# Attention layer of a fused two-block kernel: the query and key norms take their roots in batches of four tiles, from raw tiles copied out of PSUM, and the steps of an attention unit stand further apart

## The chip, the cores and the metric

One Trainium2 chip, one of its cores. The metric is the device time of one execution of the whole program in microseconds (us), measured from the outside; the kernel before was run three times. The profile and the trace come from a fourth, profiled execution. The program is one instruction stream for each engine: TensorE (PE in the rows, its weight loads PEld), VectorE (DVE), ScalarE (ACT), GpSimd (POOL) and SyncE (SP). They run side by side and meet at semaphores only; each takes its own instructions strictly in order.

## What is computed

The reference runs two transformer blocks after each other on 256 tokens of 1024 numbers, in float32. The first has a recurrent mixer, sliding-window attention and a mixture of experts. The second has two layers: feed-forward, mixer, feed-forward, each with a residual. The mixer of its second layer is the dilated attention that the change touches. What matters of it, in short form:

```
qkv = rmsnorm(h) @ w_qkv            # 256 x 1024 times 1024 x 9216: 3 groups of q, k, v with 16 heads of 64
for g, dilation in enumerate((1, 4, 16)):
    q = q_g * rsqrt(mean(q_g ** 2, over the 64 of a head) + eps) * q_gain[g]
    k = k_g * rsqrt(mean(k_g ** 2, over the 64 of a head) + eps) * k_gain[g]
    scores = q k^T * 64 ** -0.5 + bias        # the banded keys that the group's dilation reaches
    o_g, lse_g = softmax(scores) @ v_g, logsumexp(scores)
o = sum over g of softmax_g(lse_g) * o_g
mix = o @ w_out
```

## The kernel before, in words

**The work as a whole.** Every dense layer is cut into tiles of 128 or 256 output columns. Weights come from HBM in float32, one megabyte a transfer, on SyncE's queue. ScalarE rounds each tile of weights to its high part (`hi_tile`, L324), VectorE subtracts that from the tile for the low part (`lo_tile`, L328), and TensorE multiplies high and low parts in separate passes. There are four slots of split weights (`SLOTS_W`).

**The attention layer** (`attention_mixer`, L1891) has the layer `qkv` of 72 tiles. One tile is 128 tokens by 256 output columns, that is four heads; tiles 2i and 2i + 1 share their weights and are the two halves of the tokens. A tile takes 8 chunks of three matmuls (L387, L388, L389) and stays in one of three PSUM banks. The 16 heads are worked off in four turns of four heads. A turn is 18 tiles: 12 query and key tiles (three groups, query and key, two halves of the tokens) and 6 value tiles. `query(t)` numbers the 48 query and key tiles n = 0 to 47.

**A query or key tile**, before: ScalarE squares it out of PSUM (`square`, L2007, scaled by the token's root), VectorE sums the squares of each head (`sum_squares`, L2202), ScalarE takes the root (`root`, L2011), VectorE the reciprocal (`invert_root`, L2207) and then multiplies the tile in PSUM by the token's and the head's factors (`normalise`, L2196) into one of four SBUF buffers QNR. That frees the PSUM bank: `bank_free` lets TensorE begin tile t + 3 when tile t is normalised. TensorE turns the normalised tile (`transposes`, L2096, two instructions) three tiles later, and ScalarE takes the turned tile into QK (`take`, L2001). Value tiles are copied out of PSUM by ScalarE (`take_values`, L2017, L2021).

**An attention unit** is two heads and one half of the queries; there are four in a turn. Its steps are scores (TensorE, L2106 and L2114), bias and maximum (VectorE, L2219), exp (ScalarE, L2030), scaling of the even and the odd head's weights (VectorE, L2229 and L2230), turning each (TensorE, L2125), taking each (ScalarE, L2038), weighing the values (TensorE, L2138), and for every second unit the high and low parts of the output (`out_high` on ScalarE, L2050, `out_low` on VectorE, L2242).

**What sets the order.** Nothing is scheduled by a planner: each engine's order comes out of `run_layer` (ScalarE and VectorE) and `products` (TensorE), and the steps of the attention units are put in by tables. A step's place is counted in chunks of TensorE from the start of its turn, `BEGIN + APART * q + offset`: the scores of unit 0 stand at chunk 124 (tile 15 of the turn, chunk 4), the next units 12 chunks further each. `PE_STEPS`, `DVE_STEPS` and `ACT_STEPS` (L1914 to L1916) give the offsets. The units reach over the end of their turn into tiles 0 to 4 of the next one; those of the last turn reach into the output layer `attn_out`, whose chunks come from `LAST_BEFORE`.

In `run_layer`, for each tile of this layer:

```
work(t)                       # evacuation; the steps at place 0 of VectorE follow
if t is odd: make(n + 3)      # a high split on ScalarE, a low split on VectorE
between(t)                    # steps at the middle place
if t is odd: make(n + 4)
behind(t)                     # steps at the last place
```

Both high splits of an odd tile wait for the matmuls of that tile, since these read the slots that are written.

## Time and profile before

| | us |
|---|---|
| three runs, median (lowest, highest) | 2464.3 (2457.86, 2464.69) |
| the profiled execution, its own time | 2468.32 |
| span of the profiled execution, first to last instruction | 2466.4 |
| busy in the span: TensorE | 2351.7 |
| VectorE | 1340.3 |
| ScalarE | 1010.1 |
| GpSimd | 94.8 |
| the attention layer's matmuls, first to last start | 1946.7 to 2232.2 |

The trace has a row for each instruction: its start, how long it took, the engine, the line of the program, the operation, what it writes and reads, and in brackets how long the engine had been idle and what ended that. Times of the trace count from the span's start. Table loads of ScalarE (ACT_TABLE_LOAD) have rows of their own. A row with x2 or more is a run of equal instructions. TensorE's instructions overlap: a matmul begins before the one before it ends, so the cost of many is read from their starts.

### The profile page before, as it was taken

How to read it: one execution, taken by the hardware profiler on the slowest of the kernel's cores; microseconds unless marked ns; L12 is line 12 of the kernel's file. 1: busy time of each engine (PE TensorE's matmuls, PEld its weight loads, DVE VectorE, ACT ScalarE, POOL GpSimd, SP SyncE). 2: the span in 40 equal slices, each digit the busy share in tenths (PEclk: the TensorE clock that was granted, in tenths of full speed). 3: DMA queues.
4: the chain of work that ended last, by engine and by line, in shares of the span. 5: the costliest groups of instructions: out<-in, count | busy, mean ns of one | idle time of the engine just before them, and what ended most of it. 6: DMA issues, size and time to landing. Idle time of an engine off the chain costs nothing.

```text
span 2466.4 us, 36862 instructions
## 1 busy us (share of the span) xinstructions
PE 2351.7 (95%) x13979; PEld 1647.8 (67%) x13980; DVE 1340.3 (54%) x2641; ACT 1010.1 (41%) x1832; POOL 94.8 (4%) x150
## 2 busy tenths in 40 slices
PE   6999999999999999999989999999999899999999
PEld 3777854444444444444448888888888788887888
DVE  5688752222232222223247869877777555665784
ACT  3645541111111111111136546655555576775653
POOL 1000000000000000000000000000000210011000
PEclk8999999999999999999999999999999999999999
DMA  8754679999999999999975556555555655453553
GB/s 318 250 208 151 235 287 424 426 426 425 425 425 425 425 425 425 425 425 426 426 291 188 181 179 200 175 188 175 183 188 176 188 151 157 143 162 120 176 181 121
DMA packets 279032, 673.89 MB, mean 273 GB/s; under 512 B 8884, under 2 KB 236607, under 8 KB 246016
## 3 DMA queue, kind: packets, MB, share of 16 engines
q1 hardware_dynamic: 274656, 663.60, 71.1%
q0 software_dynamic: 4256, 8.65, 1.6%
q8 instruction: 80, 1.31, 0.2%
q14 instruction: 40, 0.33, 0.0%
HBM read 670.45 MB, written 1.25 MB: 272 GB/s over the span
## 4 chain that ended last, share of the span: by engine, by line
PE 83%; DVE 6%; ACT 5%; DMA 4%; issue 3%; DVEq 0%; ACTq 0%; SPq 0%
PE PS L380 26%; PE PS L1493 17%; PE PS L381 13%; PE PS L1515 9%; PE PS L1480 5%; DMA RING<-in_moe_w 3%; PE PS L1467 2%; PE PS L387 2%; PE PS L389 2%; PE PS L388 2%; DVE WS L328 1%; ACT WS L324 1%; DVE XG L1610 1%; PE PS L798 1%; DMA RAW<-in_w_ada 1%
## 5 line engine op out<-in xcount | busy, mean ns | idle before, releaser
L380 PE MATMUL PS<-HN,WS 128*128 128x512 f32 x1952 | 707.0, 405 | 15.4 <-DVE WS L328 9.4
L328 DVE TENSOR_TENSOR WS<-RAW,WS 128x1024 fp32r<-128x1024 f32 (+1 forms) x452 | 540.9, 1205 | 172.6 <-ACT WS L324 168.9
L381 PE MATMUL PS<-HN,WS 128*128 128x256 f32 x1952 | 551.7, 283 | 0.0
L324 ACT ACTIVATE WS<-RAW 128x1024 fp32r<-128x1024 f32 (+1 forms) x452 | 465.0, 1035 | 83.2 <-PE PS L381 69.5
L1493 PE MATMUL PS<-RING,XG 128*64 128x512 f32 x2048 | 447.2, 594 | 12.3 <-DVE XG L1610 11.0
L380 PEld LDWEIGHTS PS<-HN,WS 128*128 128x128 f32 x1952 | 371.1, 190 | 111.3 <-DVE WS L328 11.6
L381 PEld LDWEIGHTS PS<-HN,WS 128*128 128x128 f32 x1952 | 373.5, 191 | 0.3
L1493 PEld LDWEIGHTS PS<-RING,XG 128*64 128x64 f32 x2048 | 148.8, 137 | 296.2 <-issue 292.1
L1616 DVE TENSOR_SCALAR GLU<-PS 128x256 f32<-128x256 f32 x64 | 27.2, 425 | 415.2 <-PE PS L1493 415.2
L380 PE MATMUL PS<-MI,WS 128*128 128x512 f32 x704 | 248.9, 399 | 0.0
L1515 PE MATMUL PS<-RING,AT 128*64 128x512 f32 x1024 | 226.8, 594 | 14.8 <-ACT AT L1389 14.8
L1382 ACT ACTIVATE SIG<-GLU 128x256 f32<-128x256 f32 x64 | 26.7, 417 | 520.9 <-DVE GLU L1616 520.9
L381 PE MATMUL PS<-MI,WS 128*128 128x256 f32 x704 | 197.7, 281 | 0.0
L387 PE MATMUL PS<-WS,HN 128*128 128x256 f32 x576 | 172.0, 299 | 7.8 <-DVE QNR L2196 4.1
L1515 PEld LDWEIGHTS PS<-RING,AT 128*64 128x64 f32 x1024 | 84.6, 137 | 136.4 <-issue 135.4
L388 PE MATMUL PS<-WS,HN 128*128 128x256 f32 x576 | 163.9, 285 | 0.0
L389 PE MATMUL PS<-WS,HN 128*128 128x256 f32 x576 | 163.7, 284 | 0.0
L380 PEld LDWEIGHTS PS<-MI,WS 128*128 128x128 f32 x704 | 132.3, 188 | 33.0
L1480 PEld LDWEIGHTS PS<-PSEL,H2K 128*128 128x128 f32 x1024 | 116.7, 192 | 25.9 <-issue 25.2
L381 PEld LDWEIGHTS PS<-MI,WS 128*128 128x128 f32 x704 | 133.0, 189 | 0.0
L1610 DVE TENSOR_TENSOR XG<-PS,SH 128x512 f32<-128x512 f32 x32 | 22.1, 692 | 200.9 <-PE PS L1480 200.9
L1480 PE MATMUL PS<-PSEL,H2K 128*128 128x64 f32 x1024 | 121.1, 276 | 0.3 <-DVE PGAT L1605 0.3
(361 smaller groups left out, 2705.2 us busy)
## 6 DMA issues: line engine op xcount, KB each, us to landing
RING<-in_moe_w SPq DMA_DIRECT2D x192, 2048.0 KB, 22.7
RAW<-in_ffn_w_in SPq DMA_DIRECT2D x88, 1024.0 KB, 5.2
RAW<-in_attn_w_qkv SPq DMA_DIRECT2D x36, 1024.0 KB, 5.2
RAW<-in_ffn_w_out SPq DMA_DIRECT2D x32, 1024.0 KB, 5.0
RAW<-in_w_ada SPq DMA_DIRECT2D x24, 1024.0 KB, 8.1
RAW<-in_w_in SPq DMA_DIRECT2D x22, 1024.0 KB, 5.3
RAW<-in_ffn_w_out SPq DMA_DIRECT2D x16, 768.0 KB, 4.3
RAW<-in_conv_w_in SPq DMA_DIRECT2D x12, 1024.0 KB, 5.2
```

The costliest lines, as they stand in the source:

```text
L324: act_f(split_tile(0, n), raw_tile(n), ACT.Copy).then_inc(hi_done, 1)
L328: vec.tensor_tensor(split_tile(1, n), raw_tile(n), split_tile(0, n).bitcast(f32), ALU.subtract).then_inc(lo_done, 1)
L380: nc.tensor.matmul(both, hi[:, k, :], x2[:, :, kx, :], start=start, stop=False)
L381: ins = nc.tensor.matmul(half, lo[:, k, :], x2[:, 0, kx, :], start=False, stop=stop)
L387: nc.tensor.matmul(half, xh, w2[:, 0], start=start, stop=False)
L388: nc.tensor.matmul(half, xh, w2[:, 1], start=False, stop=False)
L389: ins = nc.tensor.matmul(half, xl, w2[:, 0], start=False, stop=stop)
L1467: nc.tensor.matmul(bank[COMB[m]][:, :], PGT[64 * g:64 * g + 64, tt * P:(tt + 1) * P], YE[64 * g:64 * g + 64, :], start=True, stop=True).th ...
L1480: last = nc.tensor.matmul(bank[4][:, k * SLOTS:(k + 1) * SLOTS], H2K[:, tt, k * P:(k + 1) * P], PSEL[:, tt, :], start=tt == 0, stop=tt == ...
L1493: last = nc.tensor.matmul(bank[j][64 * side:64 * side + 64, :], XG[:, 2 * q + k, :], w[:, k, 1024 * side + 512 * j:1024 * side + 512 * (j ...
L1515: last = nc.tensor.matmul(bank[6][64 * side:64 * side + 64, :], AT[:, b, 64 * q:64 * q + 64], w[:, b, 512 * side:512 * (side + 1)], start= ...
L1610: TTN(XG[:, :, :], bank[4][:, :].rearrange("p (k s) -> p k s", k=DC), SH2[:, :].rearrange("p (k a) -> p k a", a=1).to_broadcast([P, DC, SL ...
```

## The change

- Before, each query or key tile had its own root and its own reciprocal, of 4 columns each. Now four tiles make a batch (`BATCH = 4`), with one root and one reciprocal of 16 columns (`roots`, `invert_roots`).
- VectorE copies a tile out of PSUM as soon as its matmuls are done (`take_raw`), scaled by the token's root; that frees the bank. ScalarE squares the copy, in SBUF, in `between`, and VectorE sums in `behind`. `normalise` multiplies the copy in place in SBUF by the heads' factors. There are eight QNR buffers in place of four.
- The turning of a batch that ends with tile t comes behind tile t + 1 (first half) and tile t + 2 (second half); before, each tile was turned three tiles later.
- ScalarE runs an exp of one column behind tile 12 of each turn.
- The offsets of a unit's steps grow: the key turns by 2 chunks, the weighing by 3, the scalings by 1, the copies by 2, the output parts by 3. The scores, bias and exp stay.

```diff
-        QNR = [rg(f"QNR{i}", [S]) for i in range(4)]
-        QST = rg("QST", [4, 4])
-        QSI = rg("QSI", [2, 4])
-        RSE = rg("RSE", [TT])
+        QNR = [rg(f"QNR{i}", [S]) for i in range(2 * BATCH)]
+        QST = rg("QST", [2, BATCH, 4])
...
-        PE_STEPS = {"scores": 0, "turn_even": 12, "turn_odd": 15, "weigh": 20}
-        DVE_STEPS = {"bias": 0, "scale_even": 8, "scale_odd": 10, "out_low": 23}
-        ACT_STEPS = {"exp": 5, "take_even": 13, "take_odd": 16, "out_high": 22}
+        PE_STEPS = {"scores": 0, "turn_even": 14, "turn_odd": 17, "weigh": 23}
+        DVE_STEPS = {"bias": 0, "scale_even": 9, "scale_odd": 11, "out_low": 26}
+        ACT_STEPS = {"exp": 5, "take_even": 15, "take_odd": 18, "out_high": 25}
...
+        def batch_end(t):
+            n = query(t)
+            return n // BATCH if n is not None and n % BATCH == BATCH - 1 else None
+
+        def turned_at(s):
+            j, first = batch_end(s - 1), 0
+            if j is None:
+                j, first = batch_end(s - 2), BATCH // 2
+            return [] if j is None else [BATCH * j + first + i for i in range(BATCH // 2)]
...
-                pe.wait_ge(sem("q_normed"), n + 1)
+                pe.wait_ge(sem("q_raw"), n + 1)
...
-            def square(n, t):
+            def square(n):
                 if n >= 2:
                     act.wait_ge(sem("q_summed"), n - 1)
-                act.wait_ge(mm_done, qkv.end[t])
-                act_f(QSQ[n % 2][:, :], tile_bank(qkv, t), ACT.Square, scale=RSE[:, t % 2:t % 2 + 1]).then_inc(sem("q_sq"), 1)
-
-            def root(n):
-                act.wait_ge(sem("q_summed"), n + 1)
-                act_f(QST[:, n % 4, :], QST[:, n % 4, :], ACT.Sqrt, bias=EPSC[:, 0:1]).then_inc(sem("q_root"), 1)
+                act.wait_ge(sem("q_raw"), n + 1)
+                act_f(QSQ[n % 2][:, :], QNR[n % (2 * BATCH)][:, :], ACT.Square, scale=HD ** -0.5).then_inc(sem("q_sq"), 1)
+
+            def roots(j):
+                act.wait_ge(sem("q_summed"), BATCH * (j + 1))
+                st = QST[:, j % 2, :, :]
+                act_f(st, st, ACT.Sqrt, bias=EPSC[:, 0:1]).then_inc(sem("q_root"), 1)
...
             def behind(s):
-                n = query(s - 3)
-                if n is not None:
+                for n in turned_at(s):
                     take(n)
                 c, w = turn_and_tile(s)
                 if c >= 0:
                     for kind, q in ACT_AT.get((w, 1), ()):
                         step(c, kind, q)
+                j = batch_end(s)
+                if j is not None:
+                    roots(j)
 
             def between(s):
                 n = query(s)
                 if n is not None:
-                    root(n)
+                    square(n)
+                if s % TURN_TILES == TURN_Q:
+                    act_f(STAT[:, 6, 0:1], EPSC[:, 0:1], ACT.Exp)
...
-                n = query(s - 3)
-                if n is not None:
+                for n in turned_at(s):
                     transposes(n)
...
-            def normalise(n, t):
-                dve.wait_ge(sem("q_inverse"), n + 1)
-                if n >= 4:
-                    dve.wait_ge(sem("q_T"), n - 3)
-                heads = "p (h d) -> p h d"
-                STT(QNR[n % 4][:, :].rearrange(heads, h=4), tile_bank(qkv, t).rearrange(heads, h=4), token_root(t),
-                    QSI[:, n % 2, :].rearrange("p (h a) -> p h a", a=1).to_broadcast([P, 4, HD]),
-                    ALU.mult, ALU.mult).then_inc(sem("q_normed"), 1)
+            def normalise(n):
+                raw = QNR[n % (2 * BATCH)][:, :].rearrange("p (h d) -> p h d", h=4)
+                dve.wait_ge(sem("q_inverse"), n // BATCH + 1)
+                dve.wait_ge(sem("q_raw"), n + 1)
+                TTN(raw, raw, QST[:, n // BATCH % 2, n % BATCH, :].rearrange("p (h a) -> p h a", a=1).to_broadcast([P, 4, HD]),
+                    ALU.mult).then_inc(sem("q_normed"), 1)
+
+            def take_raw(n, t):
+                if n >= 2 * BATCH:
+                    dve.wait_ge(sem("q_T"), n - 2 * BATCH + 1)
+                dve.wait_ge(mm_done, qkv.end[t])
+                TS(QNR[n % (2 * BATCH)][:, :], tile_bank(qkv, t), token_root(t), None, ALU.mult).then_inc(sem("q_raw"), 1)
...
             def behind(s):
-                steps_at(s, 2)
                 n = query(s)
                 if n is not None:
-                    invert_root(n)
+                    sum_squares(n)
+                steps_at(s, 2)
+                j = batch_end(s - 1)
+                if j is not None:
+                    for n in range(BATCH * j + BATCH // 2, BATCH * (j + 1)):
+                        normalise(n)
 
             def work(t):
...
-                n = query(t - 1)
-                if n is not None:
-                    normalise(n, t - 1)
+                j = batch_end(t - 1)
+                if j is not None:
+                    invert_roots(j)
+                    for n in range(BATCH * j, BATCH * j + BATCH // 2):
+                        normalise(n)
                 n = query(t)
                 if n is not None:
-                    sum_squares(n)
+                    take_raw(n, t)
```

How the engines' orders move at the places of which the prediction speaks (no times in them; L numbers are the lines of the version shown, those of the new one differ by up to 24):

**VectorE, quiet tiles, before**: query tiles 6 and 7 of turn 0 (`L2202` the sum, `L2207` the reciprocal, `L2196` the multiplication out of PSUM, `L328` the two low splits behind the odd tile).

```order
L2202 TENSOR_REDUCE QST<-QSQ_168 128x4 [waits q_sq]
L2207 RECIPROCAL QSI<-QST 128x4 [waits q_root]
L2196 SCALAR_TENSOR_TENSOR QNR_172<-PS,RSC,QSI 128x256 [waits q_T,q_inverse]
L2202 TENSOR_REDUCE QST<-QSQ_169 128x4 [waits q_sq]
L328 TENSOR_TENSOR WS<-RAW_66,WS 128x1024 [waits hi_done] x2
L2207 RECIPROCAL QSI<-QST 128x4 [waits q_root]
L2196 SCALAR_TENSOR_TENSOR QNR_173<-PS,RSC,QSI 128x256 [waits q_T,q_inverse]
```

**VectorE, the same place, now**: `L2214` is the raw copy, `L2220` the sum, `L2226` the batch's reciprocal, `L2207` the multiplication in SBUF. QNR_177 holds tile 7, the last of its batch.

```order
L2214 TENSOR_SCALAR QNR_177<-PS,RSC 128x256 [waits mm_done]
L328 TENSOR_TENSOR WS<-RAW_66,WS 128x1024 [waits hi_done] x2
L2220 TENSOR_REDUCE QST<-QSQ_169 128x4 [waits q_sq]
L2226 RECIPROCAL QST<-QST 128x16 [waits q_root]
L2207 TENSOR_TENSOR QNR_174<-QNR_174,QST 128x256 [waits q_raw,q_inverse]
L2207 TENSOR_TENSOR QNR_175<-QNR_175,QST 128x256 [waits q_raw,q_inverse]
L2214 TENSOR_SCALAR QNR_170<-PS,RSC 128x256 [waits mm_done,q_T]
L2220 TENSOR_REDUCE QST<-QSQ_168 128x4 [waits q_normed,q_sq]
L2207 TENSOR_TENSOR QNR_176<-QNR_176,QST 128x256 [waits q_raw,q_inverse]
```

The sum of tile 7 has moved from ahead of the two low splits to behind them; the batch's reciprocal and multiplications come after it.

**TensorE behind tile 8 of turn 0, before**: the turning of tile 5 (QNR_171), between the last matmuls of tile 8 and the first of tile 9.

```order
L388 MATMUL PS<-WS,HN 128x256
L389 MATMUL PS<-WS,HN 128x256
L2096 MATMUL PS<-SM,QNR_171 128x128 [waits q_taken,q_normed]
L2096 MATMUL PS<-SM,QNR_171 128x128
L387 MATMUL PS<-WS,HN 128x256 [waits q_normed]
```

**TensorE behind tile 8, now**: the turning of tiles 4 and 5 (QNR_174, QNR_175), the first half of the batch that ends with tile 7.

```order
L389 MATMUL PS<-WS,HN 128x256
L2109 MATMUL PS<-SM,QNR_174 128x128 [waits q_taken,q_normed]
L2109 MATMUL PS<-SM,QNR_174 128x128
L2109 MATMUL PS<-SM,QNR_175 128x128 [waits q_taken,q_normed]
L2109 MATMUL PS<-SM,QNR_175 128x128
L387 MATMUL PS<-WS,HN 128x256 [waits q_raw]
```

Two tiles are turned there in place of one, and both wait for multiplications that need the sum of tile 7, which is one tile back.

**ScalarE where turn 0 runs into turn 1 (tiles 18 to 21), before**: `L2038` takes turned weights, `L2007` squares, `L2030` is the exp, `L2011` the root.

```order
L2038 ACTIVATE ETX_179<-PS 128x384 [waits b_pv,b_T]
L2007 ACTIVATE QSQ_168<-PS,RSE 128x256 [waits mm_done,q_summed]
L2011 ACT_TABLE_LOAD
L2011 ACTIVATE QST<-QST,EPSC 128x4 [waits q_summed]
L2038 ACTIVATE ETX_180<-PS 128x384 [waits b_pv,b_T]
L2030 ACT_TABLE_LOAD
L2030 ACTIVATE ES_177,STAT<-ES_177,STAT 128x384 [waits b_max] x2
L2050 ACTIVATE OXB<-PS 128x256 [waits b_pv]
L2007 ACTIVATE QSQ_169<-PS,RSE 128x256 [waits mm_done,q_summed]
L324 ACTIVATE WS<-RAW_68 128x1024 [waits mm_done,raw_loaded3]
L2011 ACT_TABLE_LOAD
L2011 ACTIVATE QST<-QST,EPSC 128x4 [waits q_summed]
```

**ScalarE, the same place, now**: `L2050` takes turned weights, `L2018` squares the raw copy, `L2042` is the exp, `L2062` the output's high part, `L2023` the batch's root.

```order
L324 ACTIVATE WS<-RAW_68 128x1024 [waits mm_done,raw_loaded3]
L2042 ACTIVATE ES_180,STAT<-ES_180,STAT 128x384 [waits b_max] x2
L2050 ACTIVATE ETX_182<-PS 128x384 [waits b_pv,b_T]
L2018 ACTIVATE QSQ_168<-QNR_176 128x256 [waits q_raw,q_summed]
L2050 ACTIVATE ETX_181<-PS 128x384 [waits b_pv,b_T]
L324 ACTIVATE WS<-RAW_65 128x1024 [waits mm_done,raw_loaded0]
L2018 ACTIVATE QSQ_169<-QNR_177 128x256 [waits q_raw,q_summed]
L2050 ACTIVATE ETX_182<-PS 128x384 [waits b_pv,b_T]
L324 ACTIVATE WS<-RAW_65 128x1024 [waits mm_done,raw_loaded0]
L2023 ACT_TABLE_LOAD
L2023 ACTIVATE QST<-QST,EPSC 128x16 [waits q_summed]
```

The table loads between the exps are gone; one stands ahead of the batch's root. The copy of the odd head's weights has moved behind the exp of the next unit.

## Rows read from the trace of the kernel before

**Rows 1.** Busy time by stretch: us of it, each engine busy, PEclk, DMA, GB/s.
```profile
1967.00:2001.00 34.00, 34.00 (x288) 34.00 (x287) 22.67 (x38) 22.69 (x45) 0.00 (x0) 1.00 0.51 162
...
2074.00:2115.00 41.00, 34.52 (x358) 30.87 (x357) 22.63 (x54) 30.98 (x57) 10.31 (x16) 1.00 0.56 142
```

**Rows 2.** Timeline, quiet tiles: start us, us, engine, line, operation [idle before].
```profile
1977.78 0.38 PE L2096 MATMUL PS<-SM,QNR 128*128 128x128 f32 x2
...
1978.12 0.28 PE L388 MATMUL PS<-WS,HN 128*128 128x256 f32 x1
...
1980.87 0.38 PE L2096 MATMUL PS<-SM,QNR 128*128 128x128 f32 x2
...
1978.04 0.47 ACT L2007 ACTIVATE QSQ<-PS,RSE 128x256 f32<-128x256 f32 x1 [0.74 <-PE PS L389]
...
1978.41 1.05 ACT L324 ACTIVATE WS<-RAW 128x1024 fp32r<-128x1024 f32 x1
...
1979.36 0.29 ACT L2011 ACTIVATE QST<-QST,EPSC 128x4 f32<-128x4 f32 x1
...
1979.49 2.37 DVE L328 TENSOR_TENSOR WS<-RAW,WS 128x1024 fp32r<-128x1024 f32 x2 [0.53 <-ACT WS L324]
```

**Rows 3.** Timeline, start of the attention layer, the first tile's chain.
```profile
1957.70 0.17 DVE L2265 RECIPROCAL RSC<-RSC 128x2 f32<-128x2 f32 x1 [6.28 <-ACT RSC L2073]
...
1958.61 0.42 DVE L2202 TENSOR_REDUCE QST<-QSQ 128x4 f32<-128x256 f32 x1 [0.54 <-ACT QSQ L2007]
...
1959.06 0.30 ACT L2011 ACTIVATE QST<-QST,EPSC 128x4 f32<-128x4 f32 x1 [0.49 <-DVE QST L2202]
...
1959.39 0.18 DVE L2207 RECIPROCAL QSI<-QST 128x4 f32<-128x4 f32 x1 [0.36 <-ACT QST L2011]
...
1959.60 0.48 DVE L2196 SCALAR_TENSOR_TENSOR QNR<-PS,RSC,QSI 128x256 f32<-128x256 f32 x1
...
1960.14 0.58 PE L387 MATMUL PS<-WS,HN 128*128 128x256 f32 x1 [4.11 <-DVE QNR L2196]
```

**Rows 4.** One line's instructions (L427): ns min/median/max.
```profile
L427 DVE TENSOR_TENSOR DXT<-PS,DXT x8: 414/420/440, 2252.3 to 2270.8; 128x256 f32<-128x256 f32 x8
```

**Rows 5.** Groups by line, 1940 to 2240: busy us, mean ns, idle before.
```profile
L2030 ACT ACT_TABLE_LOAD x10 | 12.8, 1283 | 0.2
```

**Rows 6.** Timeline, TensorE and ScalarE at the end of turn 1.
```profile
2074.19 0.70 PE L2106 MATMUL PS<-QK 64*128 64x256 f32 x4
...
2079.00 1.28 ACT L2030 ACT_TABLE_LOAD   x1
...
2080.30 0.61 ACT L2030 ACTIVATE ES<-ES,STAT 128x384 f32<-128x384 f32 x1
...
2081.72 0.55 PE L2125 MATMUL PS<-SM,EN 128*128 128x128 f32 x3 [0.90 <-DVE EN L2230]
...
2084.39 0.55 PE L2125 MATMUL PS<-SM,EN 128*128 128x128 f32 x3 [1.06 <-DVE EN L2230]
...
2087.82 0.89 PE L2138 MATMUL PS<-ETX,VV 128*64 128x128 f32 x16 [1.09 <-issue]
...
2096.22 0.89 PE L2138 MATMUL PS<-ETX,VV 128*64 128x128 f32 x16 [1.18 <-ACT ETX L2038]
...
2107.69 0.55 PE L2125 MATMUL PS<-SM,EN 128*128 128x128 f32 x3 [1.46 <-DVE EN L2230]
```

**Rows 7.** Gaps of TensorE, and stretches behind gaps with their granted clock.
```profile
1484.73 0.50 PE L380 MATMUL PS<-HN,WS 128*128 128x512 f32 x1 [1.90 <-DVE WS L328]
...
1485.00:1491.00 6.00, 6.00 (x36) 5.25 (x36) 5.83 (x11) 2.79 (x5) 0.00 (x0) 1.00 0.56 175
...
2285.05 0.50 PE L380 MATMUL PS<-HN,WS 128*128 128x512 f32 x1 [1.75 <-DVE WS L328]
...
2285.00:2291.00 6.00, 5.96 (x25) 5.17 (x26) 5.90 (x10) 5.10 (x10) 0.00 (x0) 0.72 0.48 160
...
1960.00:1966.00 6.00, 5.86 (x30) 5.86 (x31) 4.33 (x9) 2.79 (x6) 0.00 (x0) 0.55 0.98 200
```

22 lines of the change are left out of this document (11 added, 11 removed).

## The prediction

> **What bounds the kernel now.** I read the views in this order: busy time by stretch of the attention layer, the timeline of TensorE, ScalarE and VectorE in a quiet stretch of it, then the timeline at the end of a turn, then the granted clock behind long gaps of TensorE.
>
> The layer has 72 tiles, 18 to a turn. In the stretches where only query, key and value tiles run, TensorE has no gap at all; in the 41 us around a turn's end, where the four attention units are threaded in, it is busy 34.52 us and idle 6.48, and ScalarE is busy 30.98 [rows 1]. So a quiet tile costs its matmuls, and any new wait of TensorE there is paid in full; at a turn's end there is something to gain, three times (a fourth end runs into the output layer).
>
> A quiet tile with its two transposes takes 1980.87 - 1977.78 = 3.09 us; the two transposes take 0.21 of it (three matmuls are 0.36 apart, eight times: 2.88) [rows 2]. After an odd tile ScalarE squares it and makes two high splits, 0.95 apart, and VectorE's low splits start 1.08 after the high ones and take 1.18 each in a row [rows 2].
>
> **The new wait, step by step.** A batch ends on an odd tile (3, 7, 11 of a turn). Its root waits for the fourth sum of squares. In the new order VectorE takes that sum behind both low splits, and ScalarE's square stands between the two high splits. Half of the batch is to be turned right behind the next tile, one tile later; before, a tile was turned three tiles later. With zero at the square's start behind the odd tile (1978.04), from [rows 2]: first high split at 0.0, square at 0.95, second high split 0.37 later at 1.32 (in the row behind the square the next one starts 0.37 later), its low split 1.08 later at 2.40 (the first runs 1.08 to 2.26), the sum 1.18 later at 3.58. From the chain at the layer's start [rows 3]: sum to root 0.45, root to reciprocal 0.33, reciprocal to normalise 0.21, normalise to TensorE 0.54. The root of 16 columns and the reciprocal of 16 are taken as those of 4. The multiplication is VectorE's on 256 elements, 0.42 us, and not the 0.48 of today's three-operand form [rows 3, 4], so 0.48 to TensorE. The first multiplication starts at 3.58 + 0.45 + 0.33 + 0.21 = 4.57, the second some 0.4 later, at 4.97; TensorE can turn that tile at 5.45 and is through at 5.66. Without a wait TensorE comes to the first transposes at 1977.78 + 2.88 = 1980.66, which is 2.62, and is through both at 3.04. **The wait is 2.6 us for each batch.** Behind it on TensorE's queue stands the next tile, and nothing can pass. On ScalarE the next square and the copies of turned tiles are queued behind the waiting root, on VectorE the next raw copy behind the reciprocal; TensorE asks for that bank only two tiles later. The other half of the batch is normalised while that tile runs (2.88 us) and costs nothing. There are 12 batches; three of them end in a turn's overlap and are counted there. 9 x 2.6 = **+23.4 us**. Bounds: 2.0 (if splits and sum come 0.5 sooner than these spacings) to 3.0.
>
> **Copies and squares.** 48 raw copies out of PSUM, a tensor-scalar of 128x256, 0.42 us by the nearest row [rows 4], 20.2 us on VectorE; the multiplications lose 0.06 each; 36 reciprocals and 36 roots fall away. The dummy exp brings a table load of 1.28 to ScalarE behind tile 12, where it has a third of its time free. VectorE has about a third of the time free in every stretch [rows 1]. What hides all this is TensorE; the part that isn't hidden is in the chain above. The wait for a free bank now ends with the raw copy, a short step, so it isn't met in any quiet tile, as today.
>
> **The turn's end, three times.** Today the exp, root and copy instructions there alternate between two activation tables. The attention layer has 20 table loads of 1.28 us: ten before an exp [rows 5], the others before a root. The new order leaves 8: one before the first root and one before a dummy exp per turn. Of ScalarE 12 x 1.28 = 15.4 us go. The exp at 2080.30 starts 1.30 behind its load's start, and the load starts as the split before it ends [rows 6]: a switch costs 1.30 here. The Trainium skill (ScalarE: Activation LUTs, What ACT_TABLE_LOAD costs) adds a drain of about 1.38 us to each switch, about 2.66 in all. By it 12 switches would be 31.9 us of ScalarE and the sum could turn to a gain; this trace shows no such drain, so the row is used.
>
> I go through the waits of TensorE at one end, zero at the first scores (2074.19) [rows 6]. There are seven: five with a row, 0.90 + 1.06 + 1.09 + 1.18 + 1.46 = 5.69, and two small ones that make up the rest of the 6.48 [rows 1]. A wait costs its gap and some 0.16 more, since matmuls start 0.12 apart (2.88 over 24) and last 0.28 [rows 2]: 6.48 + 7 x 0.16 = 7.6 us.
> - First key turn, 0.90 idle: TensorE came there at 7.53 - 0.90 - 0.16 = 6.47 and comes now two chunks of 0.36 later, at 7.2. The exp starts where the load stood, at 4.8 and not at 6.1, so the weights are ready 1.3 sooner than 7.5 or, behind VectorE's low split, some 0.9 sooner. Gone. The second (1.06) moves by the same steps and comes down to 0.1.
> - First weighing, 1.09: exp of the second unit now stands ahead of the second copy on ScalarE, and the copy of the last value tile (0.95) still has to come. 0.9 stays.
> - Second weighing, 1.18: no table load ahead any more, but the raw copy, the square and an exp pair are ahead of its second copy. 0.6 stays.
> - The other three (1.46 and the two small ones) stood behind table loads. Gone.
> - New: the first batch of the next turn has the wait of 2.6, 0.5 longer for the last unit's copy between the two high splits, and 1.4 shorter for the key turn and the weighing that TensorE still has in that tile: 1.7. The one table load of the batch lies in front of the root while ScalarE waits for the sum.
>
> Left are 0.1 + 0.9 + 0.6 + 1.7 = 3.3, so 4.3 are gained: 3 x 4.3 = **-12.9 us**. Bounds: 1.5 (only the first two waits go) to 6.
>
> **The layer's start.** The first tile's bank is now free after reciprocal and raw copy, 0.21 + 0.48 = 0.69, and not after 1960.14 - 1957.70 = 2.44 [rows 3]: 1.75 earlier. The clock there is at half for most of six microseconds (0.55) [rows 7]; the earlier start may bring it back about one reading sooner, some 0.6 more. **-2.4 us** (1.7 to 3.4). **The last end** gains the first waits (2.4) and loses about 0.9 in the tail, where an exp pair now comes ahead of the third unit's second copy: **-1.5 us** (-3 to +1). Steps of the units set further apart issue the same instructions, no DMA is moved, and the bias loads on GpSimd keep their waits.
>
> So far 23.4 - 12.9 - 2.4 - 1.5 = +6.6 us.
>
> **The clock.** The other term is TensorE's granted clock. Behind a gap of 1.75 us it fell from 2.4 to 1.2 GHz for part of the next 6 us (mean 0.72), behind one of 1.90 it stayed at 1.00 [rows 7]; behind the gap of 1.46 at a turn's end it stayed too (mean of the stretch 1.00) [rows 1, 6]. One fall costs (1 - 0.72) x 6 = 1.7 us. A wait of 2.6 is longer than these three and shorter than the 4.11 behind which it did fall [rows 3, 7]. I take six falls in nine: 6 x 1.7 = **+10.2 us**; bounds none and twelve (0 to 20).
>
> Sum: +16.8 us, on the profiled execution 2468.3 + 16.8 = 2485.1. That execution (span 2466.4) lies 4.0 above the median of the three runs, 2464.3; on the median the sum gives **2481.1 us**.
>
> **The rivals.**
> - *The waits come, the clock holds.* For: 1.90 and 1.46 without a fall. Against: 1.75 with one, and each new wait is longer. +6.6: 2470.9 us, no difference that can be told. Chance 0.15.
> - *Every wait is followed by a fall, or the turn's end gives back little.* For: the two long gaps; the new wait there. Twelve falls give +20.4 for +10.2: 2491.3; with only 1.5 gained at each end and six falls, 2489.5. Chance 0.22.
> - *Faster: the batch's chain fits into one tile.* If the second multiplication of a batch ended within about 2.5 us of the odd tile's end, TensorE would not wait, and nothing would fall: -12.9 - 2.4 - 1.5 = -16.8, 2447.5 us. The point that decides is VectorE's sum behind the second low split. That split can't start before 2.4, as its high split waits for the odd tile and each takes 0.95, so the rows speak against it. Chance 0.05.
> - *The change doesn't do what it says.* If the tables still alternated at a turn's end, nothing would be gained there and the time would be 2481.1 + 12.9 + 1.5 = 2495.5; the new order shows eight loads, so this is left in the second rival.
>
> **How the numbers follow.** My case has 0.58. About 0.3% (7.4 us) is what a measurement can tell from no change. Slower by more: my case and the second rival, less the part of my case with the fewest falls and better ends: 0.79. Within: the first rival and that part: 0.16. Faster: 0.05. The range goes from the first rival with a good turn's end (2466) to the second with waits of 3.0 (2496).
>
> **What would show it.** Right: a gap of TensorE of about 2.4 us before the first transposes of each batch, at tiles 4, 8 and 12 of a turn, ended by VectorE's multiplication; the stretch of quiet tiles longer by 5 us or more a turn; the turn's end shorter by about 4; eight table loads; readings of the clock at 0.5 behind some of those gaps. Wrong: transposes that find their tiles normalised, gaps of under 1 us there, or a clock at 1.00 throughout the layer.

## The result, and the profile after

The changed kernel takes 2478.83 us (median of seven runs, 2477.67 to 2483.9), the kernel before, in seven runs on the same chip, 2464.3. The ratio is 1.0064, 95% interval 1.0052 to 1.0076: 14.5 us slower. The profiled execution took 2478.83 as well, with a span of 2477.0; its head shows less ScalarE (983.2 for 1010.1) and more TensorE, mostly the same work at a lower clock (0.987 for 0.991).

```profile
PE 2359.1 (95%) x13982; PEld 1654.5 (67%) x13983; DVE 1351.4 (55%) x2652; ACT 983.2 (40%) x1788; POOL 95.2 (4%) x150
```

A turn of the attention layer, from the first scores of turn 2 to those of turn 3, grew from 73.0 to 75.0 us, the first turn from 41.0 to 51.5, and the layer, from the first matmul behind its start to the start of the last unit's weighing, from 289.3 to 304.9.

**What TensorE waited for in the layer** (the view of waits, rows of the layer; columns: who <- whose result, us in total, times, longest). First the kernel before:

```profile
PE PS L2125 <- DVE EN L2230: 12.6, 12, 1.5
PE PS L2138 <- ACT ETX L2038: 7.1, 11, 1.2
```

and the changed one:

```profile
PE PS L2109 <- DVE QNR L2207: 24.9, 12, 2.7
...
PE PS L2151 <- ACT ETX L2050: 2.8, 4, 1.8
PE PS L387 <- DVE QNR L2214: 2.4, 1, 2.4
```

The twelve waits for scaled weights (L2125) are gone and the eleven for taken weights are down to four; in their place stand twelve waits of the query and key transposes (L2109) for the batch's multiplication, one for each batch. The wait at the layer's start is 1.7 shorter (4.11 before, [rows 3]).

**The chain behind an odd tile** that ends a batch (timeline, tile 7 of turn 0; start, duration, idle before). It answers to [rows 2].

```profile
1979.93 0.48 DVE L2214 TENSOR_SCALAR QNR<-PS,RSC 128x256 f32<-128x256 f32 x1 [0.87 <-PE PS L389]
1979.99 1.06 ACT L324 ACTIVATE WS<-RAW 128x1024 fp32r<-128x1024 f32 x1 [1.38 <-PE PS L389]
1980.96 0.40 ACT L2018 ACTIVATE QSQ<-QNR 128x256 f32<-128x256 f32 x1
1981.09 2.48 DVE L328 TENSOR_TENSOR WS<-RAW,WS 128x1024 fp32r<-128x1024 f32 x2 [0.67 <-ACT WS L324]
1981.27 1.05 ACT L324 ACTIVATE WS<-RAW 128x1024 fp32r<-128x1024 f32 x1
1983.48 0.41 DVE L2220 TENSOR_REDUCE QST<-QSQ 128x4 f32<-128x256 f32 x1
1983.93 0.31 ACT L2023 ACTIVATE QST<-QST,EPSC 128x16 f32<-128x16 f32 x1 [1.62 <-DVE QST L2220]
1984.27 0.25 DVE L2226 RECIPROCAL QST<-QST 128x16 f32<-128x16 f32 x1 [0.37 <-ACT QST L2023]
1984.56 0.76 DVE L2207 TENSOR_TENSOR QNR<-QNR,QST 128x256 f32<-128x256 f32 x2
1985.04 0.77 PE L2109 MATMUL PS<-SM,QNR 128*128 128x128 f32 x4 [2.27 <-DVE QNR L2207]
```

The square was done at 1980.96 + 0.40 = 1981.36. Its sum starts at 1983.48, since both low splits (2.48 us) are ahead of it on VectorE's queue.

**The clock** (windows; span of the window, busy time of PE, PEld, DVE, ACT, POOL, then PEclk, DMA share, GB/s) behind two of the nine quiet waits, the first at 1985.04, the second at 2001.52, both with a gap of 2.27:

```profile
1984.50:1988.50 4.00, 3.46 (x20) 3.33 (x21) 2.27 (x7) 1.15 (x3) 0.00 (x0) 0.72 0.80 262
2001.50:2005.50 4.00, 3.98 (x33) 3.85 (x34) 0.96 (x3) 2.12 (x5) 0.00 (x0) 1.00 0.74 252
```

Behind five of the nine the clock fell to 1.2 GHz, each time for 3.4 us of readings at 0.5; behind four, and behind the 1.31 at each turn's end, it stayed at 2.4 GHz. The five are the layer's first batch (1968.58) and the second batch of every turn (1985.04, 2060.02, 2135.13, 2210.09); behind a turn's third batch, with the same gap, it never fell. At half clock for 3.4 us TensorE does 1.7 us less work, so five falls cost 5 x 1.7 = 8.5 us by this reckoning.

**The turn's end** (windows as in [rows 1], and timeline as in [rows 6]):

```profile
2084.00:2125.00 41.00, 39.13 (x397) 35.70 (x396) 24.80 (x60) 25.50 (x53) 10.31 (x16) 1.00 0.63 168
```

```profile
2084.95 0.70 PE L2119 MATMUL PS<-QK 64*128 64x256 f32 x4
...
2096.82 0.89 PE L2151 MATMUL PS<-ETX,VV 128*64 128x128 f32 x16 [0.39 <-issue]
...
2104.25 0.89 PE L2151 MATMUL PS<-ETX,VV 128*64 128x128 f32 x16 [0.18 <-ACT ETX L2050]
...
2120.17 0.77 PE L2109 MATMUL PS<-SM,QNR 128*128 128x128 f32 x4 [1.31 <-DVE QNR L2207]
2120.69 0.36 PE L387 MATMUL PS<-WS,HN 128*128 128x256 f32 x1
```

TensorE is idle for 1.87 of 41 us, for 6.48 before. From the first scores to the first matmul of the next turn's tile 5 (in both kernels two query tiles are turned on the way) it takes 2120.69 - 2084.95 = 35.74; before it was 2114.63 - 2074.19 = 40.44. An end gives back 4.7.

**The sum.** Nine quiet waits of 21.0 us of gaps (24.9 less three of 1.31) and 9 x 0.16: +22.5. Three ends: -14.1. Falls of the clock: +8.5. The half-clock stretch at the layer's start lasts 3.4 us for 6.8, of which TensorE was idle for the first 1.6: -0.9. The last end, from its first scores to its last weighing, 28.33 for 29.25: -0.9. That makes +15.1 in the layer, where 304.86 - 289.25 = 15.6 is measured; with the start's gap (-1.7) it is +13.4 beside the 14.5 of the medians. The two profiled executions differ by 10.5 us only, because the rest of the program, which the change does not touch, was 3.2 us faster in that one execution (and the layer's start gap 1.7 shorter).

### The profile page after: what moved, and what is told of

Same layout as the page of the kernel before. It is cut to its first block, busy times and chain, and to the rows that moved or that the text cites. A ratio compares the mean times of both kernels' runs of the same rounds, so it can differ in the third digit from the quotient of the medians.

```text
span 2477.0 us, 36921 instructions
## 1 busy us (share of the span) xinstructions
PE 2359.1 (95%) x13982; PEld 1654.5 (67%) x13983; DVE 1351.4 (55%) x2652; ACT 983.2 (40%) x1788; POOL 95.2 (4%) x150
## 3 DMA queue, kind: packets, MB, share of 16 engines
q8 instruction: 80, 1.31, 0.2%
## 4 chain that ended last, share of the span: by engine, by line
PE 81%; DVE 7%; ACT 5%; DMA 4%; issue 3%; DVEq 0%; ACTq 0%; SPq 0%
PE PS L380 26%; PE PS L1493 17%; PE PS L381 13%; PE PS L1515 9%; PE PS L1480 5%; DMA RING<-in_moe_w 3%; PE PS L1467 2%; PE PS L387 2%; PE PS L389 2%; PE PS L388 2%; DVE WS L328 2%; ACT WS L324 1%; DVE XG L1610 1%; PE PS L798 1%; DMA RAW<-in_w_ada 1%
## 5 line engine op out<-in xcount | busy, mean ns | idle before, releaser
L328 DVE TENSOR_TENSOR WS<-RAW,WS 128x1024 fp32r<-128x1024 f32 (+1 forms) x452 | 542.4, 1205 | 177.8 <-ACT WS L324 173.2
L1493 PE MATMUL PS<-RING,XG 128*64 128x512 f32 x2048 | 447.2, 594 | 12.1 <-DVE XG L1610 11.0
L387 PE MATMUL PS<-WS,HN 128*128 128x256 f32 x576 | 174.8, 304 | 6.0 <-DVE WS L328 3.6
L388 PE MATMUL PS<-WS,HN 128*128 128x256 f32 x576 | 167.7, 291 | 0.0
L389 PE MATMUL PS<-WS,HN 128*128 128x256 f32 x576 | 167.5, 291 | 0.0
## 6 DMA issues: line engine op xcount, KB each, us to landing
RING<-in_moe_w SPq DMA_DIRECT2D x192, 2048.0 KB, 22.5
```

The lines of the kernel that those rows point to most:

```text
L328: vec.tensor_tensor(split_tile(1, n), raw_tile(n), split_tile(0, n).bitcast(f32), ALU.subtract).then_inc(lo_done, 1)
L387: nc.tensor.matmul(half, xh, w2[:, 0], start=start, stop=False)
L388: nc.tensor.matmul(half, xh, w2[:, 1], start=False, stop=False)
L389: ins = nc.tensor.matmul(half, xl, w2[:, 0], start=False, stop=stop)
L1493: last = nc.tensor.matmul(bank[j][64 * side:64 * side + 64, :], XG[:, 2 * q + k, :], w[:, k, 1024 * side + 512 * j:1024 * side + 512 * (j ...
```

## The experiments

My theory: batching by itself is worth several microseconds at the turns' ends; the loss is the wait of TensorE behind every batch, because the turning stands one tile behind the batch's last tile, and the clock that falls behind it. The rivals: the raw copies and the square out of SBUF slow the engines down; or the larger offsets do. All ratios are to the kernel before, run on the same chip in the same set; "turn" is the length of a turn in the profile, defined as above.

| kernel | median us (lowest, highest; runs) | ratio, 95% | turn | layer |
|---|---|---|---|---|
| before | 2464.3 | | 73.0 | 289.3 |
| the change | 2478.83 (2477.67, 2483.9; 7) | 1.0064 [1.0052, 1.0076] | 75.0 | 304.9 |
| 1 turned a tile later | 2446.48 (2440.73, 2452.39; 5) | 0.9944 [0.9924, 0.9963] | 68.6 | 277.2 |
| 2 old offsets | 2490.56 (2484.14, 2493.45; 4) | 1.0123 [1.0106, 1.014] | 76.7 to 77.9 | 310.8 |
| 3 offsets only | 2463.93 (2459.2, 2470.76; 9) | 1.001 [0.9995, 1.0025] | 72.3 to 73.1 | 288.4 |
| 4 sum ahead | 2465.38 (2457.94, 2471.15; 10) | 1.0005 [0.9991, 1.002] | 72.0 to 73.5 | 292.2 |
| 5 = 1, takes early | 2448.1 (2447.44, 2454.27; 4) | 0.9947 [0.9929, 0.9965] | 67.9 | 274.2 |
| 6 = 1 + old offsets | 2454.52 (2449.26, 2456.27; 6) | 0.9956 [0.9939, 0.9974] | 69.7 | 280.1 |
| 7 = 1, no dummy exp | 2454.34 (2450.21, 2464.18; 7) | 0.9968 [0.9951, 0.9985] | 69.9 | 282.6 |
| 8 gap filled | 2468.41 (2467.17, 2476.93; 10) | 1.0026 [1.0012, 1.004] | 73.5 to 73.7 | 297.5 |
| 9 = 7 + table loads | 2477.32 (2474.84, 2485.19; 4) | 1.0069 [1.0049, 1.0088] | 75.3 to 79.6 | 306.1 |
| 10 = 5 again | 2444.76 (2439.9, 2451.04; 6) | 0.9931 [0.9914, 0.9947] | 67.9 | 274.1 |
| 11 = 1 again | 2450.24 (2445.88, 2454.99; 6) | 0.9951 [0.9936, 0.9967] | 68.6 | 277.2 |
| 12 = 2 again | 2484.01 (2478.2, 2488.82; 6) | 1.0088 [1.0072, 1.0104] | 78.2 | 313.8 |

### 1. The batch turned one tile later

```diff
-            j, first = batch_end(s - 1), 0
+            j, first = batch_end(s - 2), 0
             if j is None:
-                j, first = batch_end(s - 2), BATCH // 2
+                j, first = batch_end(s - 3), BATCH // 2
```

> The changed kernel with each half of a batch turned one tile later (behind tiles 5 and 6 in place of 4 and 5, and so on). My theory (the batch's chain ends 2.3 to 2.7 us after TensorE comes to the transposes, one tile of 2.9 us covers it): the 12 gaps before the transposes go, and with them the falls of the clock behind them: 9 x 2.4 + 3 x 1.5 = 26 us, and five falls of 1.7, together 31 to 36 us less than the changed kernel, 2443 to 2449. Rival (the gaps only move, since the square or the bank comes late next): less than 10 us less. Rival (the cost lies in the copies and the longer order on VectorE): the time stays within 5 us of the changed kernel.

Measured: ratio 0.9944. By the ratios that is 1.2% or some 29 us faster than the change (32 by the medians; 31 to 36 were expected), and 14 us faster than before. The view of waits, in the layer:

```profile
PE PS L2109 <- issue: 3.1, 6, 0.7
...
PE PS L2109 <- ACT QK L2012: 1.8, 2, 1.0
...
PE PS L2109 <- DVE QNR L2207: 0.2, 1, 0.2
```

The wait for the multiplication went from 24.9 us to 0.2, and the ends kept their gain (the layer is 12.1 shorter than before). Raw copy, square out of SBUF and multiplication in SBUF are all still in this kernel, so the first rival falls: apart from these 0.2 us, the only wait of TensorE that ends with one of them is the raw copy's at the layer's start, which is shorter than before. What is left at L2109 is 4.9 us (3.1 and 1.8), six gaps of up to 0.7 among it. One of them in the timeline:

```profile
2047.13 1.04 ACT L324 ACTIVATE WS<-RAW 128x1024 fp32r<-128x1024 f32 x1
...
2048.08 0.82 ACT L2012 ACTIVATE QK<-PS,QKG 128x256 f32<-128x256 f32 x2
...
2048.63 0.78 PE L2109 MATMUL PS<-SM,QNR 128*128 128x128 f32 x4 [0.70 <-issue]
```

The bank that this turning writes is freed by ScalarE's copy of the half turned before it, and that copy stands behind a high split. The bracket names "issue"; that it is this copy is read from 2048.08 + 0.47 = 2048.55, and experiment 5 tries it.

### 2. The old offsets, in the changed kernel

```diff
-        PE_STEPS = {"scores": 0, "turn_even": 14, "turn_odd": 17, "weigh": 23}
+        PE_STEPS = {"scores": 0, "turn_even": 12, "turn_odd": 15, "weigh": 20}
...
```

(the tables of VectorE and ScalarE likewise)

> The changed kernel with the three tables of offsets as before (key turns 2 chunks, weighing 3 chunks earlier). My theory: with the table loads gone, the larger offsets are worth one or two waits at each turn's end (the first key turn found its weights ready because it stands two chunks later), 0.5 to 1.5 us at each of four ends, so 2 to 6 us slower than the changed kernel; the gaps before the transposes stay at 2.3. Rival (the offsets are what gained at the turns' ends, the table loads nothing): 10 us or more slower. Rival (the offsets cost in the tail): 1 to 3 us faster.

Measured: ratio 1.0123, 14 us slower than the change by the ratios, more than twice what I had allowed. Experiment 12 repeats it. The view of waits shows the batch's wait as before and new ones at the ends:

```profile
PE PS L2109 <- DVE QNR L2207: 24.7, 12, 2.7
...
PE PS L2151 <- issue: 3.3, 3, 1.1
PE PS L2151 <- ACT ETX L2050: 2.5, 5, 0.6
PE PS L2138 <- DVE EN L2249: 2.5, 5, 0.5
```

These three are 8.3 us of gaps. In the changed kernel the waits of weighing and key turning of these kinds are 3.6: the offsets save about 5 us of them. In this execution the clock fell behind six of the nine quiet waits, where the changed kernel had five falls. The second rival falls: the offsets are worth something, and more with the batches than without.

### 3. The new offsets alone, in the kernel before

```diff
-        PE_STEPS = {"scores": 0, "turn_even": 12, "turn_odd": 15, "weigh": 20}
+        PE_STEPS = {"scores": 0, "turn_even": 14, "turn_odd": 17, "weigh": 23}
...
```

> The kernel before with the new offsets alone; roots and table loads as before. My theory (the waits at a turn's end come from the table loads on ScalarE): the same within 4 us as the kernel before, since the loads still stand ahead of the exps. Rival (the offsets alone make the gain at the turns' ends of 4 us each): 8 to 15 us faster than the kernel before.

Measured: ratio 1.001, interval 0.9995 to 1.0025: no difference. Most of the waits moved instead of going away, from the turning of the keys (12.6 to 4.3) to the weighing (7.1 to 13.8):

```profile
PE PS L2138 <- ACT ETX L2038: 13.8, 8, 2.4
PE PS L2125 <- DVE EN L2230: 4.3, 4, 1.1
```

The longest of them, in the timeline of ScalarE and TensorE:

```profile
2085.23 1.28 ACT L2011 ACT_TABLE_LOAD   x1
...
2086.84 1.28 ACT L2030 ACT_TABLE_LOAD   x1
2088.14 0.61 ACT L2030 ACTIVATE ES<-ES,STAT 128x384 f32<-128x384 f32 x1
...
2089.35 0.47 ACT L2038 ACTIVATE ETX<-PS 128x384 f32<-128x384 f32 x1
2089.87 0.89 PE L2138 MATMUL PS<-ETX,VV 128*64 128x128 f32 x16 [2.38 <-ACT ETX L2038]
```

With the tables still alternating, two loads and an exp pair stand ahead of the copy at the weighing's new place too.

All waits of the two steps together went from 24.1 us to 19.3, so a part did go away. The clock took it back: it fell behind this gap (2091.26 to 2094.67 at half) and behind the gap of 2.38 a turn later (2162.94), which no turn of the kernel before has. The one turn without a fall is 72.3 long, 0.7 less than before; the two with one are 72.8 and 73.1.

### 4. The last sum ahead of one low split

In the changed kernel `sum_squares(n)` moves from VectorE's `behind` to `between`, so that one low split stands ahead of it and not two:

```diff
             def between(s):
...
+                n = query(s)
+                if n is not None:
+                    sum_squares(n)
                 steps_at(s, 1)
 
             def behind(s):
-                n = query(s)
-                if n is not None:
-                    sum_squares(n)
                 steps_at(s, 2)
```

> The changed kernel with VectorE's sum of squares between the two low splits, in place of behind both. My theory: the root can then run as soon as ScalarE has made its second high split, so the second low split is out of ScalarE's way but still ahead of the reciprocal on VectorE: the reciprocal starts right behind the low split, 0.8 to 0.9 us sooner (sum 0.41, root 0.31 and the hand-overs fall out of the chain), the gaps shrink from 2.3 to about 1.4, 12 of them, 9 to 11 us faster than the changed kernel and some falls of the clock fewer. Rival (the wait is set by ScalarE's splits, not by the sum's place): gaps as before, no change.

Measured: ratio 1.0005, 13.4 us less than the change by the medians. The wait is shorter by 0.59, less than the 0.8 to 0.9 expected, and the clock falls once where it fell five times:

```profile
1975.99 0.41 DVE L2220 TENSOR_REDUCE QST<-QSQ 128x4 f32<-128x256 f32 x1
1976.32 1.22 DVE L328 TENSOR_TENSOR WS<-RAW,WS 128x1024 fp32r<-128x1024 f32 x1
1976.44 0.31 ACT L2023 ACTIVATE QST<-QST,EPSC 128x16 f32<-128x16 f32 x1 [0.37 <-DVE QST L2220]
1977.45 0.25 DVE L2226 RECIPROCAL QST<-QST 128x16 f32<-128x16 f32 x1
1978.21 0.78 PE L2109 MATMUL PS<-SM,QNR 128*128 128x128 f32 x4 [1.68 <-DVE QNR L2207]
```

The root is early, but its reciprocal now waits behind the second low split, and a gap of 1.68 stays. In the view of waits the 24.9 became 18.2, 6.7 less; four falls fewer are 6.8 less; together 13.5 (the layer is 12.7 shorter). So it is the order on VectorE's queue that makes the wait as long as it is.

### 5 and 10. Turned later, and the copies of turned tiles ahead of the splits

On top of experiment 1, behind odd tiles ScalarE takes the turned tiles in the middle place, ahead of its second high split:

```diff
             def behind(s):
-                for n in turned_at(s):
-                    take(n)
+                if s % 2 == 0:
+                    for n in turned_at(s):
+                        take(n)
...
             def between(s):
                 n = query(s)
                 if n is not None:
                     square(n)
+                if s % 2:
+                    for n in turned_at(s):
+                        take(n)
```

> The run with the batch turned one tile later, and on odd tiles ScalarE's copies of the turned tiles ahead of its second high split, in place of behind it. My theory (what is left there, gaps of 0.70 to 0.75 before the second half's transposes, is TensorE waiting for those copies): these gaps go, some 5 to 6 us less than the run without it, about 2441. Rival (those gaps wait for VectorE's multiplications): no change, or worse, since the second split comes 0.8 later.

> The fastest candidate again, beside the run without its last edit on the same chip: 2 to 4 us less than that one (the attention layer of its profile was 3.0 us shorter), 2444 to 2448. Rival: no difference.

Measured: 0.9947 and 0.9931. The gaps of about 0.7 are gone, which shows what they waited for, but the layer is only 3.0 us shorter than in experiment 1, where 5 to 6 and a time of 2441 were expected. Part of the difference is a new wait: ahead of four groups of scores TensorE now waits for the copies of turned tiles.

```profile
PE PS L2123 <- ACT QK L2012: 1.7, 4, 0.5
```

In run times the two kernels, side by side on one chip, are 2444.76 and 2450.24, and the intervals of their ratios overlap, so the step from one to the other is shown by the layer and not by the times. This is the fastest version: 16 and 19 us below the kernel before by its two medians, 13 and 17 by its ratios. Another part of its cost is unexplained: a tile behind which four transposes follow takes 3.73 us,

```profile
1979.17 0.78 PE L2113 MATMUL PS<-SM,QNR 128*128 128x128 f32 x4
...
1982.90 0.78 PE L2113 MATMUL PS<-SM,QNR 128*128 128x128 f32 x4
```

where in the changed kernel a tile and the second half of a batch take 2005.35 - 2002.05 = 3.30 from one first matmul to the next, and the four transposes 0.60. Turning the tiles of a half one by one was not tried.

### 6. Turned later, with the old offsets

The edits of experiments 1 and 2 together.

> The batch turned one tile later with the three tables of offsets as before. With this the four cases of roots (single or batched) and offsets (old or new) stand side by side without the batch's wait. My theory (the batch takes the table loads away, and the offsets are worth something only with it): 4 to 7 us slower than with the new offsets, and still 10 us or more faster than the kernel before: 2449 to 2454. Rival (the offsets are what gains): no faster than the kernel before.

Measured: ratio 0.9956, turn 69.7, layer 280.1. With the three kernels before, this makes a square of turn lengths: single roots 73.0 with the old offsets and 72.3 to 73.1 with the new; batches turned later 69.7 with the old and 68.6 with the new. The kernel with the roots in batches gains 3.3 us a turn with the old offsets, and the new offsets add 1.1. With single roots they give 0.7 in the one turn without a fall (experiment 3). The run times are not clear enough to tell this kernel from experiment 1: its interval, 0.9939 to 0.9974, overlaps with 0.9924 to 0.9963. The 2.9 us between them, where 4 to 7 were expected, are read from the layer's length.

### 7. Turned later, without the dummy exp

```diff
-                if s % TURN_TILES == TURN_Q:
-                    act_f(STAT[:, 6, 0:1], EPSC[:, 0:1], ACT.Exp)
```

> The batch turned one tile later, without the exp of one column behind tile 12, so that the exp table is loaded ahead of the first unit's exp. My theory (a table load on ScalarE there delays the first unit by 1.3 us, and with it the first two key turns): a gap of 0.4 to 1.0 in front of each of two key turns at each of four ends, 3 to 6 us slower. Rival (a single load a turn is hidden): the same within 2 us.

Measured: ratio 0.9968, turn 69.9, layer 282.6, 5.4 longer than in experiment 1 (1.3 in each turn and 1.6 at the last end). There are still eight table loads; the one before the exps now stands in the first unit's path, and the key turns wait four times, once at each end:

```profile
PE PS L2136 <- DVE EN L2247: 4.3, 4, 1.1
```

### 9. The table loads put back, in the kernel of experiment 7

One column of a root ahead of the exps of units 2 and 3, in the first three turns; nothing reads it:

```diff
             def exp(c, q):
...
+                if q >= 2 and c < TURNS - 1:
+                    act_f(STAT[:, 6, 0:1], EPSC[:, 0:1], ACT.Sqrt)
```

> The run without the dummy exp (batch turned one tile later), with a root of one column ahead of the exps of the third and fourth unit in the first three turns: 20 table loads in the attention layer again, as in the kernel before, with the work of the batch kept. My theory (the waits at a turn's end in the kernel before came from the table loads): each end gets 3 to 5 us longer, 9 to 15 us slower than the run without the dummy exp, about the time of the kernel before, 2462 to 2468. Rival (the batch's other savings on ScalarE, 36 roots and the shorter square, made the gain): within 4 us of the run without the dummy exp.

Measured: 2477.32 us against 2454.34 in experiment 7, with 20 table loads in place of 8: 23 us by the medians and 25 by the ratios (the chips differ), more than the 9 to 15 that I expected. Each pair of loads stands right ahead of an exp pair and of the copy behind it:

```profile
2011.12 1.28 ACT L2040 ACT_TABLE_LOAD   x1
2012.41 0.20 ACT L2040 ACTIVATE STAT<-EPSC 128x1 f32<-128x1 f32 x1
2012.62 1.28 ACT L2044 ACT_TABLE_LOAD   x1
2013.91 0.61 ACT L2044 ACTIVATE ES<-ES,STAT 128x384 f32<-128x384 f32 x1
```

```profile
PE PS L2151 <- ACT ETX L2052: 19.0, 8, 3.1
```

The weighings' waits are 16.3 us longer than in experiment 7 (2.7), and most of the rest of the layer's 23.5 is the clock, which fell behind four of the six gaps that end with such a copy (from 2.37 to 3.12 us), for one reading of 3.4 us each and once for two. The kernel before had its loads at easier places, so this says more about the pattern than about what they cost there. The 3.3 us a turn of experiment 6 is a better measure of the batching as a whole, but it does not separate the loads from the 36 roots and reciprocals that fell away with them; how much of the gain is the loads' alone is not shown. The Trainium skill (ScalarE: Activation LUTs, Table sets: the hidden batching unit) advises to put the exps together and the roots together; this case agrees: 12 more loads cost 23 us here.

### 8. The batch's wait filled with matmuls

In the changed kernel TensorE runs matmuls on data that is there, into the bank of the next tile, which that tile's first matmul starts afresh, instead of standing idle; 17 of them in a quiet place, 8 at a turn's end. This is added work, and the wait stays as long as it was.

```diff
                 for n in turned_at(s):
+                    if n % BATCH == 0:
+                        qkv.bank_free(pe, s + 1)
+                        for _ in range(8 if n >= 12 and n % 12 == 0 else 17):
+                            nc.tensor.matmul(tile_bank(qkv, s + 1), HN[:, 0, 0, 0:P], HN[:, 0, 0, :], start=True, stop=True)
                     transposes(n)
```

> The changed kernel with matmuls of no use (17 of 128x256, 8 at a turn's end) ahead of each batch's first transposes, into the bank of the next tile, where TensorE would have waited; nothing is left out of the computation, and the waits for the batch stay as long as they are. My theory (a part of the loss, 1.7 us each for about five falls, is the clock and not the wait): no reading of the clock at 0.5 behind the batches, 7 to 10 us faster than the changed kernel, about 2470. Rival (the falls cost nothing since TensorE waits anyway): no change. If the added matmuls outlast the wait it is slower instead.

Measured: 2468.41 us, 10.4 less than the change by the medians, and 9.4 by the ratios. The longest wait at L2109 is 1.0 and no reading in the layer is at 0.5 behind any batch:

```profile
1977.81 0.88 PE L2177 MATMUL PS<-HN 128*128 128x256 f32 x6
1978.91 0.77 PE L2109 MATMUL PS<-SM,QNR 128*128 128x128 f32 x4 [0.23 <-DVE QNR L2211]
...
1962.00:2013.00 51.00, 49.51 (x429) 47.38 (x428) 30.71 (x59) 28.52 (x55) 0.83 (x2) 1.00 0.42 133
```

Useless work made the kernel faster. With the waits held and the falls taken away, the loss against before shrinks from 1.0064 to 1.0026, so the clock is some six tenths of it (the intervals leave room for three to nine tenths); in the layer's length it is 7.4 of 15.6.

### 11 and 12. Two kernels again

> The batch turned one tile later, again, for the comparison on one chip: 2446 to 2450.

> The changed kernel with the old offsets again, since its median was 11.7 us above the changed kernel where its profile had the layer only 6 us longer. If the waits explain it, 2484 to 2487 in most runs; if it has more falls of the clock, behind waits that are there in both, in some executions, single runs spread from 2484 to 2494 and their granted clock is below 0.987.

Experiment 1 again: 0.9951 for 0.9944, the same. Experiment 2 again: 1.0088 for 1.0123. In the view of waits its rows for the batches, the key turns and the weighings are those of experiment 2, to the tenth. In its profiled execution eight falls followed the batches' waits, in experiment 2's six, where the changed kernel had five; the layers are 313.8 and 310.8 long. So the number of falls is not a property of the kernel alone. The old offsets cost some 5 us of waits in the changed kernel; what is above that differed between the two sets of runs (14 and 6 us by the ratios). The falls do not explain this difference: the execution with eight is the shorter one as a whole (2479.04 us for 2484.14), by what ran outside the layer. The runs without a profile fit neither of the two expected pictures: they spread from 2478.2 to 2488.8.

## Why the prediction was right, and where it was off

The forecast was 2481.1 us, the measured median is 2478.83. It came true by its own mechanism, term by term:

- **The new wait, 9 x 2.6 = +23.4.** Measured +22.5. The chain was forecast with the sum at 3.58 behind the odd tile's end, the first multiplication at 4.57 and TensorE at 5.05 or, waiting for the second tile, 5.45. In the trace, from the start of the first high split at 1979.99, the sum starts at 3.49, the multiplication at 4.57 and TensorE at 5.05. The 0.09 that the sum was early went to the root, the reciprocal of 16 columns (0.25, not 0.18, so 0.29 to the multiplication) and their hand-overs. TensorE did not stop for the second tile. Experiment 1 shows that this wait hangs on the distance between batch and turning, experiment 4 that it hangs on the low splits.
- **The turn's end, 3 x -4.3 = -12.9.** Measured 3 x -4.7 = -14.1. The waits left were forecast as 0.1, 0.9, 0.6 and 1.7; they are 0, 0.39, 0.18 and 1.31 of gap. The two copies came earlier than I had them. I named the table loads as the cause; experiment 3 shows that the offsets alone give at most 0.7 a turn, and 6 that the batches alone give three quarters, but not whether it is their loads or their fewer roots.
- **The layer's start, -2.4.** The gap is 1.70 shorter (forecast 1.75) and the half-clock stretch is one reading shorter, worth 0.9 (0.6). Experiment 3 agrees: there too the stretch was one reading, and the first turn is 40.2 us for 41.0. Such a reading is not always paid for: experiments 1 and 11 are one kernel, the first had no half clock at the layer's start and the second one reading, and their first turns are both 43.1. Where the clock held, TensorE waited 0.9 for a low split instead.
- **The last end, -1.5.** Measured -0.9. The tail's cost is there as forecast: a gap of 1.82 before the third unit's weighing, since the exp pair is ahead of its copy,

```profile
2246.75 0.47 PE L380 MATMUL PS<-OXB,WS 128*128 128x512 f32 x1 [1.46 <-issue]
...
2260.89 0.89 PE L2151 MATMUL PS<-ETX,VV 128*64 128x128 f32 x16 [1.82 <-ACT ETX L2050]
```

  but the 1.46 before the output layer's first matmul I had not seen. It is there in experiments 1, 3, 4 and 5 as well, and not with the old offsets, so it belongs to the offsets; what it waits for was not traced. The prediction also says that steps set further apart issue the same instructions. They do not quite: the last units' steps that fall behind the third tile of `attn_out` are issued by `last_turn` and then once more by `last_inside`. Before, three key turns and two weighings were done twice (105 matmuls of L2125 where 16 units need 96), now four and two (108). The change adds one repeated key turn, three matmuls; both kernels pay for the others.
- **The clock, six falls of nine, +10.2.** Measured five, +8.5. Experiment 8 gives the term by itself: 9.4 to 10.4 of run time, 7.4 in the layer's length. Why the same gap of 2.27 is followed by a fall in some places and not in others stays open; a count of six was a choice between two observed behaviours, and a good one by luck as much as by reason, as the six and eight falls of one kernel in experiments 2 and 12 show.
- **The rest at nothing.** Copies, squares and the shorter root work cost no time of TensorE that experiment 1 shows.

Against the forecast sum of +16.8 the terms measured +13.4 (one fall fewer 1.7, ends 1.2, quiet waits 0.9, start 0.2, less 0.6 at the last end), and the medians +14.5; the 1.1 between the terms and the medians has no place in the trace. The rival on the faster side had its point of decision in the right place: the sum behind the second low split. It did not come true in this kernel. With the turning one tile later, where that sum no longer decides, the medians are 2446 and 2450 us (2450 and 2452 by the ratios), near that rival's sum (2447.5).

## What to carry to other kernels

Before several short steps are gathered into one, write down the chain from the last member of the group to its first consumer, with everything that stands ahead on the in-order queues, and compare it with the distance at which the consumer is placed: here the batching was worth 3.3 us a turn, and it lost 14.5 us in all because the consumer was not moved one tile further away. When TensorE is the bound, count a new gap of the length seen here (2.3 to 2.7 us) for itself and for the clock that may fall behind it. Changes that pay more together (loads removed, steps set apart) have to be tried together as well as alone, and a gain in waits can be hidden by a fall of the clock, so both are to be counted.

## What was not expected of the hardware

- Gaps of the same length were not followed by the same clock: of nine waits from 2.27 to 2.72 us in one execution five were followed by 3.4 us at 1.2 GHz, in two executions of a kernel with the same waits six (experiment 2) and eight (experiment 12) were. Behind gaps of 1.31 none was.
- The longer gap was not the one that was followed: in experiment 9 the clock stayed at 2.4 GHz behind 3.08 us (2173.55), and fell behind 1.82 us ahead of a weighing in the output layer (2252.69), for 6.8 us. Behind that same gap of 1.82 it also fell in experiments 3 and 7, and not in the changed kernel or in experiments 1, 4, 5 and 8.
- Filling those gaps with matmuls whose results nobody reads saved 9 to 10 us of 2479.
- The raw copy out of PSUM with a per-token factor takes 0.48 us in all 48 cases, like the three-operand form before ([rows 3]), and not 0.42 as the two-operand one ([rows 4]).
- No drain was seen around a table load: in experiment 9 the load starts at 2012.62, 0.21 behind the start of a one-column operation that takes 0.20, and its exp starts 1.29 later. The Trainium skill (ScalarE: Activation LUTs, What ACT_TABLE_LOAD costs) adds about 1.38 us of drain to a load; the measurement decides.
- Four transposes in a row took 0.60 us in one place (the changed kernel, 2004.99) and 0.78 in another of the same shape (experiment 5), where ten gaps of about 0.2 stand ahead of such transposes whose end the profile does not name.
